# Two edits of a hand-made order on VectorE: expert picks behind the residual norm, 17 gathered rows earlier, and eight rows between digits and picks

## The chip, the core and the metric

The kernel runs on one core of one Trainium2 chip. The metric is device time in microseconds (us); lower is better. The engines are TensorE (PE in the profile; its weight loads are PEld), VectorE (DVE), ScalarE (ACT), GpSimd (POOL) and SyncE (SP), each with its own instruction stream, tied by semaphores.

## The reference

One decoder layer over 1024 tokens of width 1024. A mixer (causal pooling and a short gated convolution, one input projection and one output projection) is followed by a product-key expert retrieval:

```python
q = (xn @ w_query).reshape(T, 8, 2, 128)
s = einsum('thpc,hpkc->thpk', q, sub_keys)          # 128 keys per half
s1, i1 = top_k(s[:, :, 0], 16);  s2, i2 = top_k(s[:, :, 1], 16)
cand_s = s1[..., :, None] + s2[..., None, :]        # 256 pairs per head
top_s, pos = top_k(cand_s, 16);  idx = take_along_axis(cand_i, pos)
gates = softmax(top_s)
out[t] = sum over 8 heads x 16 picks of  gate * gelu(expert_u[idx] . x[t]) * expert_v[idx]
```

There are 16384 experts with a row of 1024 floats (4 KB) in each of expert_u and expert_v. Every token uses 128 of them.

## The kernel before

**Tokens.** Eight tiles of 128 tokens, ranked two at a time. The mixer and the queries run in four periods n = 0 to 3 of 256 tokens (two tiles each). Period n also ranks, on VectorE, the two tiles of period n - 1 (ranks 0 and 1 in period 1, 2 and 3 in period 2, 4 and 5 in period 3). Tiles 6 and 7 are ranked in the last part.

**Two ways to apply the experts.** Four tiles (ranks 0, 3, 6, 7) are gathered: for each of the 128 picks GpSimd issues one indirect DMA that fetches 128 rows of 4 KB (512 KB) into one of eight ring slots (L679), and VectorE consumes it in one unit called "row": a dot product for u rows (L1186), a multiply-add for v rows (L1197). There are 1024 rows, in the order of `ROWS`: u0, u1, v0, ... Gather r waits until row r - 8 is used. The other four tiles are dense: TensorE multiplies them with all experts (L785 scores, L831 sums, with the gate tables in between). Of these the tile of rank 1 has its gates scattered into the tables in HBM by 128 indirect DMAs of GpSimd (L650): heads 0 to 2 behind the gather `rows_by[1] + 7`, heads 3 to 7 behind the gather `rows_by[2] + 7`. `rows_by[n]` is how many rows stand in VectorE's order up to the end of period n.

**A tile's ranking on VectorE** is the list keys x4, cands, pairs x2, digits, pick, keep. "digits" (L1111 to L1130) prepares; ScalarE then makes 16 place masks (L864, `pick_places`), at a point of its own order that the planner fixes; "pick" (L1136 to L1144) waits for them (`hot_ready`); "keep" writes the expert numbers (L1170), which lets the gathers of a tile start, or the routes (L1165).

**The order on VectorE in a period.** The work of the mixer is written out, and between its steps stand places named conv0 to conv3, gate, y, y2, outp, query. `FILL[n]` gives each place an amount of us. `take(us)` fills it with the next ranking units by their `COST`, and with rows where the next unit is a pick less than 10 us (`PLACES_US`) behind its digits, or no ranking unit is left. So a period's list is fixed when the kernel is built; nothing is reordered on the chip. The steps of the mixer around it, in VectorE's order: pool_windows (L1302), conv g (L1317) with a fill ahead of each and add_x (L1335) behind the third, norm_x of the next period (L1273, L1277), conv_gate (L1343), fill gate, conv_gate, fill y, add_y (L1349, L1351), fill y2, roots_y (L1360), the residual add_half 0 and 1 (L1377), fill outp, add_half 2 and 3, norm_h x2 (L1382, L1387), fill query. TensorE's order in a period is bcv 0 to 4 (L699), the sum of squares of the next period (L710, waits for add_x), bcv 5, pa 0 and 1 of the next period (L717, waits for norm_x), pool (L728), outp 0 and 1 (L742, wait for conv_gate through ScalarE's L912), ynorm (L733, waits for add_y), outp 2 and 3, pa 2 and 3, the transposes (L748, wait for norm_h), the queries (L699), the scores (L769). It has four pairs of PSUM banks: a step also waits until the step four before it is emptied.

In the kernel before, the planner's lists are: period 1, outp: pick of tile 0; query: keep 0, keys 1 x2, cands, pairs x2, digits 1, rows 0 to 7, pick 1, keep 1, rows 8 to 10, spread (normalises the gates of the scattered tile), rows 11 to 18. Period 2, outp: pick 2; query: keep 2, keys 3 x2, cands, pairs x2, digits 3, rows 19 to 26, pick 3, keep 3, rows 27 to 39. Period 3, query: digits 4, keys 5 x4, pick 4, keep 4, cands, pairs x2, digits 5, route, rows 40 to 46, pick 5, keep 5. `rows_by` is 0, 19, 40, 47.

**Behind the periods** come 48 batches that build the gate tables, and then the dense part. There VectorE's list `order` is made of two lists: `late` (the rankings of tiles 6 and 7 with the other 977 rows between them, then weights, totals, finishes) and `items` (128 "gate" units, L1252, and 128 "sum" units, L1258, in the order in which TensorE needs them). The items are spread over `late` in proportion to its cost. `digits` is held back until the next three items are sums, or until its own pick comes.

Of the kernel before, what the change touches and what calls it, by code (L numbers as in the profile page):

```python
# [75 lines left out]


FILL = [[(f"conv{g}", 4.0) for g in range(4)] + [("gate", gate), ("y", y), ("y2", y2), ("outp", outp), ("query", query)]
        for gate, y, y2, outp, query in ((0.0, 0.0, 0.0, 0.0, 0.0), (4.0, 13.0, 6.0, 2.0, 66.0), (4.0, 13.0, 6.0, 2.0, 66.0), (0.0, 8.0, 0.0, 0.0, 66.0))]
HOT_FILL = 0.0  # L80
DENSE_SPEED = 0.99
FIRST_FILL = 42.0
# [3 lines left out]
def program(nc, hT, x_rows, w_all, sub_keys, pool_w, small, rows_g, expert_u, expert_v, uT, out):  # L86
# [57 lines left out]
    with ctx:  # L144
        def sb(name, shape, dt=FP32):
            return ctx.enter_context(nc.sbuf_tensor(name, shape, dt))
# [74 lines left out]
        gate = sb("gate", [P, HK])  # L221
# [120 lines left out]


        COST = {"keys": 6.8, "cands": 1.4, "pairs": 6.2, "digits": 3.7, "pick": 5.4, "keep": 1.2, "spread": 1.5, "route": 1.0, "row": 1.35}
        PLACES_US = 10.0

        def ranking_of(r):
            return ([("keys", r, q) for q in range(4)] + [("cands", r, 0)] + [("pairs", r, q) for q in range(2)]
# [10 lines left out]
        def take(us):  # L359
# [3 lines left out]
            while spent < us:  # L363
                row_ready = rows < 2 * HK and list(GATHERED_RANK)[rows // HK] in ranked
                if to_rank and not (to_rank[0][0] == "pick" and since_digits < PLACES_US):
                    unit = to_rank.pop(0)
# [78 lines left out]

        order, done, held = [], 0, []

        first_fill = int(np.searchsorted(np.cumsum([COST.get(u[0], 0.0) for u in late]), FIRST_FILL))
        for i, (unit, c) in enumerate(zip(late, cost)):
            if i == first_fill:  # L450
                order += items[:VJ]
                done = VJ
            if unit[0] == "pick" and held:
                order.append(held.pop())
            if unit[0] == "digits":
                held.append(unit)
            else:
                order.append(unit)
            if held and done + 2 < len(items) and all(k == "sum" for k, _, _ in items[done:done + 3]):
                order.append(held.pop())  # L460
            if i < first_fill:
                continue
            share = (c - cost[first_fill]) / (cost[-1] - cost[first_fill])
            until = min(len(items), VJ + int((len(items) - VJ) * share * DENSE_SPEED))
            order += items[done:until]
            done = until
# [1051 lines left out]
```

How the kernel before makes its waits and increments, by code:

```python
        @block.sync  # L501
# [1 line left out]
            def load_x(n):  # L503
                if n >= 2:
                    sp.wait_ge(pe_step, full(("query", n - 2, 3)))
                    if DENSE_OF[n - 2]:
                        sp.wait_ge(xfT_kept[n - 2], 16 * len(DENSE_OF[n - 2]))
                sp.dma_start(xnT[n % 2][:, :, 0:GW], hT[:, :, BASE[n] + META:BASE[n] + COLS]).then_inc(xT_loaded[n], 16)
# [3 lines left out]
            def load_w():  # L513
                k = loads[0]
                loads[0] += 1
                if k >= WSLOTS:
                    _, by, count = uses[k - WSLOTS]
                    sp.wait_ge(pe_step if by == "step" else w_freed, count)
                sp.dma_start(wslot[k % WSLOTS].rearrange("p k n -> p (k n)"), w_all[uses[k][0], :, :]).then_inc(w_loaded[k % WSLOTS], 16)
# [7 lines left out]
            sp.dma_start(poolw.rearrange("p g n -> p (g n)"), pool_w).then_inc(const_in, 16)  # L527
            sp.dma_start(skT, sub_keys).then_inc(const_in, 16)
            sp.dma_start(g_ffn, rows_g[:, 0:D]).then_inc(const_in, 16)
            for n in range(GRPS):
                for i in range(20 if n + 1 < GRPS else 18):
                    load_w()
                    if i == 0 and 2 <= n + 1 < GRPS:
                        load_x(n + 1)
            sp.wait_ge(pe_step, LAST_STEP)
            for n in range(GRPS):
                if DENSE_OF[n]:
                    sp.wait_ge(xfT_kept[n], 16 * len(DENSE_OF[n]))
# [144 lines left out]
        @block.tensor  # L685
        def _(pe):
            pe.wait_ge(const_dve, 2)
            pe.wait_ge(const_pool, 2)
```

## Time and profile before

| | |
|---|---|
| median of 3 timed runs | 2552.13 us (2550.41 to 2559.08) |
| the profiled execution | 2544.61 us, span 2542.9 us |
| TensorE busy | 2468.2 us (97%) |
| VectorE busy | 1975.3 us (78%) |
| GpSimd busy | 1438.6 us (57%) |
| ScalarE busy | 424.2 us (17%) |
| moved by DMA | 857.68 MB, 337 GB/s over the span |

A busy share is a mean over parts with different limits. The periods run from 0 to about 636 us, the table batches to about 792 us, and the dense part from 833.65 us to the end. The time between the profiled execution and its span is 1.7 us.

### The profile page before, as it was taken

The page shows a single profiled execution, that of the slowest core. Times are in us where ns is not written, and L with a number is a line of the kernel's source. Part 1 is how long each engine was busy: PE and PEld are TensorE (multiplying, and loading weights), DVE is VectorE, ACT ScalarE, POOL GpSimd, SP SyncE. Part 2 cuts the span into 40 slices and gives each one's busy share as a digit, 9 for nine tenths or more (in the row PEclk, how much of TensorE's full clock was granted, in tenths as well). Part 3 has the DMA queues.
Part 4 walks back from the last instruction along what each step waited for, and adds up shares of the span by engine and source line. Part 5 has one row for each costly group of instructions (what it writes and reads, how often), then busy time and mean ns, then how long its engine had stood idle before and what let it go on. Part 6 is the DMA issues. An engine that isn't in the chain of part 4 may idle for free.

```text
span 2542.9 us, 24120 instructions
## 1 busy us (share of the span) xinstructions
PE 2468.2 (97%) x7561; PEld 1356.1 (53%) x7561; DVE 1975.3 (78%) x4252; ACT 424.2 (17%) x782; POOL 1438.6 (57%) x1169
## 2 busy tenths in 40 slices
PE   8999999999889999999999999999999999999998
PEld 7687886868665344444444444444444444444443
DVE  4308799768888878778798877879888787888886
ACT  0213313224984000200010000000000000000001
POOL 0000276687401467577576766767676776767673
PEclk9999999999999999999999999999999999999999
DMA  8544776864868799999999999999999999999995
GB/s 333 217 158 165 307 247 191 325 164 86 264 181 277 282 379 389 386 353 406 397 372 420 420 393 399 381 411 419 420 420 402 402 402 413 417 418 419 419 420 219
DMA packets 288079, 857.68 MB, mean 337 GB/s; under 512 B 42064, under 2 KB 99408, under 8 KB 273360
## 3 DMA queue, kind: packets, MB, share of 16 engines
q0 software_dynamic: 167184, 541.73, 55.5%
q1 hardware_dynamic: 108416, 289.25, 30.1%
q10 hardware_dynamic: 12352, 25.17, 2.6%
q8 instruction: 60, 0.98, 0.1%
q14 instruction: 67, 0.55, 0.1%
HBM read 807.75 MB, written 48.30 MB: 337 GB/s over the span
## 4 chain that ended last, share of the span: by engine, by line
PE 61%; DMA 15%; POOL 13%; issue 6%; ACT 3%; DVE 1%; SPq 1%; ACTq 0%; DVEq 0%
PE pairs L831 19%; PE pairs L785 17%; PE pairs L699 15%; POOL ring L679 13%; DMA ring<-in_expert_u,idx 7%; DMA ring<-in_expert_v,idx 6%; PE pairs L742 4%; PE pairs L717 2%; ACT arena L985 2%; PE pairs L769 1%; PE pairs L798 1%; ACT arena L1009 1%; DMA arena<-gate_tables 1%; DVE arena L1197 1%; ACT arena L987 0%
## 5 line engine op out<-in xcount | busy, mean ns | idle before, releaser
L679 POOL DMA_INDIRECT ring<-in_expert_u,idx x512 | 644.7, 1259 | 626.2 <-DVE dots L1186 355.5
L831 PE MATMUL pairs<-arena 128*128 128x512 f32 x2048 | 888.7, 595 | 15.0 <-DVE arena L1252 13.2
L785 PE MATMUL pairs<-arena 128*128 128x512 f32 x2048 | 882.5, 592 | 0.0
L1186 DVE CUSTOM_DVE_ANT_0 junk<-ring,xf 128x1024 bf16<-128x1024 f32 x512 | 612.0, 1223 | 163.4 <-DMA ring<-in_expert_u,idx 159.9
L679 POOL DMA_INDIRECT ring<-in_expert_v,idx x512 | 581.2, 1135 | 265.9 <-issue 119.9
L831 PEld LDWEIGHTS pairs<-arena 128*128 128x128 f32 x2048 | 390.5, 191 | 510.8 <-issue 507.9
L785 PEld LDWEIGHTS pairs<-arena 128*128 128x128 f32 x2048 | 388.6, 190 | 486.5 <-issue 486.5
L1197 DVE SCALAR_TENSOR_TENSOR arena<-ring,arena 128x1024 f32<-128x1024 f32 x381 | 475.6, 1284 | 96.0 <-DMA ring<-in_expert_v,idx 94.8
L699 PE MATMUL pairs<-arena 128*128 128x256 f32 (+1 forms) x1792 | 393.2, 382 | 5.9 <-ACT arena L946 4.7
L699 PEld LDWEIGHTS pairs<-arena 128*128 128x128 f32 x1792 | 341.2, 191 | 55.9 <-ACT arena L946 5.4
L993 ACT ACTIVATE arena<-pairs 128x512 f32<-128x512 f32 x128 | 76.1, 597 | 1068.0 <-PE pairs L785 1042.2
L650 POOL DMA_INDIRECT gate_tables<-gate,place x128 | 206.0, 1609 | 51.9 <-issue 38.7
L1197 DVE SCALAR_TENSOR_TENSOR xf<-ring,arena,xf 128x1024 f32<-128x1024 f32 x126 | 156.6, 1283 | 24.8 <-DMA ring<-in_expert_v,idx 24.7
L1467 DVE TENSOR_SCALAR arena<-iota,arena 128x128 f32<-128x128 f32 x384 | 101.3, 344 | 25.5 <-PE pairs L798 25.5
L798 PE MATMUL pairs<-arena 128*128 128x128 f32 x768 | 91.4, 277 | 28.0 <-ACT arena L1009 25.3
L742 PE MATMUL pairs<-arena 128*128 128x512 f32 x256 | 111.2, 592 | 0.0
L798 PEld LDWEIGHTS pairs<-arena 128*128 128x128 f32 x768 | 88.2, 192 | 34.0 <-issue 30.9
L1258 DVE TENSOR_TENSOR arena<-arena,pairs 128x512 f32<-128x512 f32 x128 | 87.0, 680 | 18.1 <-PE pairs L831 17.7
L1252 DVE TENSOR_TENSOR arena<-arena 128x512 f32<-128x512 f32 x128 | 87.5, 687 | 14.7 <-DMA arena<-gate_tables 11.6
L864 ACT ACTIVATE pick_all<-digit,place 128x256 bf16<-128x256 f32 x128 | 80.4, 721 | 51.9 <-DVE digit L1130 51.9
L742 PEld LDWEIGHTS pairs<-arena 128*128 128x128 f32 x256 | 48.6, 190 | 57.8 <-issue 55.0
L1062 DVE MAX8 tops<-arena 128x8 f32<-128x128 f32 x112 | 24.5, 280 | 62.0 <-ACT arena L961 60.4
(174 smaller groups left out, 1059.2 us busy)
## 6 DMA issues: line engine op xcount, KB each, us to landing
arena<-in_w_all SPq DMA_DIRECT2D x80, 1024.0 KB, 6.6
arena<-in_uT SPq DMA_DIRECT2D x128, 512.0 KB, 6.7
arena<-in_expert_v SPq DMA_DIRECT2D x128, 512.0 KB, 9.0
arena<-gate_tables SPq DMA_DIRECT2D x32, 1024.0 KB, 10.0
gate_tables<-arena SPq DMA_DIRECT2D x11, 2048.0 KB, 9.1
gate_tables<-junk ACTq DMA_DIRECT2D x4, 2048.0 KB, 13.8
ring<-in_expert_u,idx POOLq DMA_INDIRECT x512, 9.0
ring<-in_expert_v,idx POOLq DMA_INDIRECT x512, 9.6
```

What stands on the lines that cost most here:

```text
L650: nc.gpsimd.indirect_dma_start(out=g_flat, out_offset=bass.IndirectOffsetOnAxis(ap=place[:, k:k + 1], axis=0), in_=gate[:, k:k + 1], in_of ...
L679: nc.gpsimd.indirect_dma_start(out=ring[:, r % RING, :], out_offset=None, in_=expert_u if table == "u" else expert_v, in_offset=bass.Indir ...
L699: last = nc.tensor.matmul(out_, w[:, k, c * P:(c + 1) * P], xn[:, k, :], start=(k == 0), stop=(k == KD - 1))
L742: last = nc.tensor.matmul(pair[:, q * 512:(q + 1) * 512], yT[:, NG * (1 - half) + k, t * P:(t + 1) * P], w_out[q].rearrange("p k n -> p (k ...
L785: last = nc.tensor.matmul(score_bank[x], uslot[:, x % USLOTS, k * P:(k + 1) * P], xfT[:, k, :], start=(k == 0), stop=(k == KD - 1))
L798: last = nc.tensor.matmul(g_bank[(2 * b + m) % 4][:, q * KEYS:(q + 1) * KEYS], hots[:, c, 0, 4 * m + q, :], hots[:, c, 1, 4 * m + q, :], s ...
L831: last = nc.tensor.matmul(o_bank[n % 4], gated[:, x % GSLOTS, t * P:(t + 1) * P], vrows[:, j, half * 512:(half + 1) * 512], start=(j == 0) ...
L1186: nc.vector.tensor_tensor_reduce(out=junk[:, r % 2, :], in0=row, in1=xf[:, t % 2, :], scale=1.0, scalar=0.0, op0=ALU.mult, op1=ALU.add, ac ...
L1197: nc.vector.scalar_tensor_tensor(out=to[:, k % 2, :], in0=row, scalar=weight[:, k:k + 1], in1=h2 if k == 0 else to[:, k % 2, :], op0=ALU.m ...
L1252: nc.vector.tensor_tensor(s, s, gtab[a // GJ % 2][:, :, a % GJ, :], ALU.mult).then_inc(w_ready, 1)
L1258: nc.vector.tensor_tensor(piece, piece, o_bank[b % 4], ALU.add).then_inc(o_added, 1)
L1467: last = nc.vector.tensor_scalar(hots[:, c, 1, t, :], iota[:], routeT[:, 1, k:k + 1], routeT[:, 2, k:k + 1], ALU.is_equal, ALU.mult)
```

## The change

Two numbers of `FILL` change in periods 1 and 2 (outp 2.0 to 0.0; query 66.0 to 82.0 and 84.0), and the loop that makes `order` holds a pick back until eight rows stand behind its digits, with its keep behind it.

```diff
 FILL = [...
-        for gate, y, y2, outp, query in ((0.0, 0.0, 0.0, 0.0, 0.0), (4.0, 13.0, 6.0, 2.0, 66.0), (4.0, 13.0, 6.0, 2.0, 66.0), (0.0, 8.0, 0.0, 0.0, 66.0))]
+        for gate, y, y2, outp, query in ((0.0, 0.0, 0.0, 0.0, 0.0), (4.0, 13.0, 6.0, 0.0, 82.0), (4.0, 13.0, 6.0, 0.0, 84.0), (0.0, 8.0, 0.0, 0.0, 66.0))]
...
-        PLACES_US = 10.0
+        PLACES_US, PLACES_ROWS = 10.0, 8
...
+        pick_late, rows_since = [], 0
...
             if unit[0] == "pick" and held:
                 order.append(held.pop())
+                rows_since = 0
+            rows_since += unit[0] == "row"
             if unit[0] == "digits":
                 held.append(unit)
+            elif unit[0] == "pick" and rows_since < PLACES_ROWS or unit[0] == "keep" and pick_late:
+                pick_late.append(unit)
             else:
                 order.append(unit)
+            if rows_since >= PLACES_ROWS:
+                order += pick_late
+                pick_late = []
             if held and done + 2 < len(items) and all(k == "sum" for k, _, _ in items[done:done + 3]):
                 order.append(held.pop())
+                rows_since = 0
```

## Rows read from the trace of the kernel before

**Rows 1.** The page: the span, and the busy time of each engine.
```profile
span 2542.9 us, 24120 instructions
PE 2468.2 (97%) x7561; PEld 1356.1 (53%) x7561; DVE 1975.3 (78%) x4252; ACT 424.2 (17%) x782; POOL 1438.6 (57%) x1169
```

**Rows 2.** Busy by window (us, PE, PEld, DVE, ACT, POOL, clock, DMA, GB/s).
```profile
834.00:2161.00 1327.00, 1324.42 (x3078) 585.20 (x3077) 1079.29 (x1714) 89.65 (x145) 903.21 (x753) 1.00 0.99 393
```

**Rows 3.** Waits of PE from 834 us: us in total, times, longest.
```profile
PE pairs L831 <- DVE arena L1252: 13.2, 6, 6.2
PE pairs L831 <- DVE arena L1258: 1.1, 1, 1.1
```

**Rows 4.** Timeline of PE, two stretches of 114 sums (start, us, idle before).
```profile
1718.75 49.16 PE L831 MATMUL pairs<-arena 128*128 128x512 f32 x114 [0.54 <-DVE arena L1252]
...
2482.85 51.70 PE L831 MATMUL pairs<-arena 128*128 128x512 f32 x114 [4.31 <-DVE arena L1252]
```

**Rows 5.** Busy by window, gathers of line 679 on POOL alone.
```profile
833.60:2482.80 1649.20, 1127.46 (x944) 1.00 1.00 398
```

**Rows 6.** Timeline of DVE, period 1: picks, residual, digits, last row.
```profile
255.33 2.28 DVE L1136 TENSOR_TENSOR pick_all<-topf,pick_all 128x4096 bf16<-128x4096 bf16 x1
...
260.99 1.28 DVE L1377 SCALAR_TENSOR_TENSOR arena<-pairs,ycol,arena 128x1024 f32<-128x1024 f32 x1
262.50 1.28 DVE L1377 SCALAR_TENSOR_TENSOR arena<-pairs,ycol,arena 128x1024 f32<-128x1024 f32 x1 [0.22 <-PE pairs L742]
...
290.91 0.29 DVE L1130 TENSOR_TENSOR digit<-pos,pick_all 128x128 f32<-128x128 uint32 x1
...
311.26 2.29 DVE L1136 TENSOR_TENSOR pick_all<-topf,pick_all 128x4096 bf16<-128x4096 bf16 x1 [10.58 <-ACT pick_all L864]
...
330.85 1.22 DVE L1186 CUSTOM_DVE_ANT_0 junk<-ring,xf 128x1024 bf16<-128x1024 f32 x1
```

**Rows 7.** Timeline of ACT: the place masks of tile 1.
```profile
301.25 9.98 ACT L864 ACTIVATE pick_all<-digit,place 128x256 bf16<-128x256 f32 x16
```

**Rows 8.** Ring, POOL, 325 to 338.6 us: ns, starts; landing.
```profile
L679 POOL DMA_INDIRECT ring<-in_expert_u,idx x8: 946/1140/1988, 325.2 to 337.4; - x8
...
DMA to landing us min/median/max: 6.2/14.7/17.3
```

**Rows 9.** Timeline of DVE, period 2: norm_x, add_y.
```profile
373.49 1.75 DVE L1273 RECIPROCAL arena<-arena 128x256 f32<-128x256 f32 x1 [1.67 <-ACT arena L927]
...
399.37 0.69 DVE L1351 TENSOR_TENSOR arena<-arena 128x512 f32<-128x512 f32 x1
```

**Rows 10.** Timeline of PE, period 2: sum of squares, ynorm.
```profile
370.88 1.03 PE L710 MATMUL pairs<-arena,ones 128*128 128x256 f32 x4
...
401.01 1.03 PE L733 MATMUL pairs<-arena,ones 128*128 128x256 f32 x4
```

**Rows 11.** Timeline of DVE: pick 3, last row, conv_gate of period 3.
```profile
465.06 2.29 DVE L1136 TENSOR_TENSOR pick_all<-topf,pick_all 128x4096 bf16<-128x4096 bf16 x1 [10.56 <-ACT pick_all L864]
...
489.45 1.23 DVE L1186 CUSTOM_DVE_ANT_0 junk<-ring,xf 128x1024 bf16<-128x1024 f32 x1 [4.01 <-DMA ring<-in_expert_u,idx]
...
532.42 0.76 DVE L1343 TENSOR_TENSOR arena<-arena 128x256 f32<-128x256 f32 x2 [3.73 <-ACT arena L935]
```

**Rows 12.** Ring, POOL, 482.8 to 493 us.
```profile
L679 POOL DMA_INDIRECT ring<-in_expert_u,idx x8: 934/938/1097, 482.9 to 491.8; - x8
...
DMA to landing us min/median/max: 7.5/7.6/7.7
```

**Rows 13.** Timeline of PE: the queries of periods 2 and 3.
```profile
426.23 55.49 PE L699 MATMUL pairs<-arena 128*128 128x256 f32 x256 [1.80 <-ACT arena L946]
...
566.45 1.94 PE L748 MATMUL pairs<-ident,arena 128*128 128x128 f32 x8 [3.76 <-DVE arena L1387]
569.55 57.24 PE L699 MATMUL pairs<-arena 128*128 128x256 f32 x256 [1.16 <-issue]
```

**Rows 14.** Timeline of DVE, dense part: pick 6.
```profile
1074.63 2.29 DVE L1136 TENSOR_TENSOR pick_all<-topf,pick_all 128x4096 bf16<-128x4096 bf16 x1 [5.72 <-ACT pick_all L864]
```

## Prediction, made before the changed kernel was run

> **What bounds the kernel now.** The page first: TensorE is busy for 97% of the span, VectorE for 78% [rows 1]. That is a mean over parts, so I split it. By windows, TensorE is busy for 1324.42 of 1327 us of the dense part from 834 to 2161 us [rows 2], and its waits from 834 us on name only VectorE's gate and sum units: 13.2 + 1.1 us, of which 6.2 us are the start of the part, where the first gates load [rows 3]. So 8.1 us are all that VectorE and the gathered rows cost TensorE in the dense part. The timeline adds one price: the longest of these waits, 4.31 us, ends at 2482.85 us, and the 114 matmuls behind it take 51.70 us where the same 114 take 49.16 us behind a wait of 0.54 us [rows 4], 2.5 us more. The dense part can give back 8.1 + 2.5 = 10.6 us, whatever happens to the rows. The rows themselves are close behind: 944 gathers in 1649.2 us, 1.75 us each [rows 5], about as long as TensorE's own list. The two lines are in step, and the rows' line has no large reserve on TensorE's.
>
> In the periods ahead of it (0 to 636 us) TensorE waits just as little, but here VectorE is the engine that is level with it. I read that from VectorE's timeline in period 2, from the end of period 1's list on. The last row of period 1 starts at 330.85 us and lasts 1.22 us, and the mixer's work of period 2 follows it at 332.0 [rows 6]. From there to add_y I find one wait, 1.67 us ahead of norm_x; add_y ends at 399.37 + 0.69 = 400.06 us [rows 9], and TensorE takes up ynorm, which needs it, at 401.01 [rows 10], 0.95 us later. (The sum of squares, at 370.88, and pa lie between and move with it.) VectorE's reserve in period 2 is 1.67 + 0.95 = 2.6 us. Any more lateness passes to TensorE, and TensorE has no idle time later in which to win it back. In period 3 the one wait is 3.73 us ahead of the conv_gate that outp needs [rows 11].
>
> **The change, part by part.**
>
> *Which units move.* I work the planner's list out by hand. With outp at 0.0 the pick of tile 0 (2) and its keep go to the head of the query list. Period 1, amount 82: 5.4 + 1.2 + 13.6 + 1.4 + 12.4 + 3.7 = 37.7 to the end of digits, 8 rows of 1.35 = 48.5, pick and keep 55.1, 3 rows and spread 60.65, then 16 rows to 82.25. That is 27 rows for 19. Period 2, amount 84: 37.7, 8 rows, pick, keep = 55.1, then 22 rows: 30 for 21. `rows_by` becomes 0, 27, 57, 64. The extra rows, 8 and 9, all stand behind the second pick of their period. None stands between a digits and its pick, where there are eight as before, because `PLACES_US` is as it was.
>
> *The pick behind the residual.* Pick 0 takes from 255.33 to 260.99 us, 5.7 us. Behind it add_half 3 still waits 0.22 us for TensorE, at 262.50 [rows 6]. So the pick fills a wait for TensorE now. Taken away, that wait grows by 5.7 us, norm_h ends where it did, and the transposes start no earlier. The 5.7 us then stand ahead of digits 1, which end at 290.91 + 0.29 + 5.7 = 296.9 us. ScalarE starts its masks at 301.25 and is done at 311.2 [rows 7], at a place of its own order that does not move. So pick 1 starts at 311.26 as before, and its wait of 10.58 us shrinks to about 4.9. The same in period 2, where pick 3 waits 10.56 us [rows 11]. This edit is worth 0. If the cover were gone it would cost 5.7 us; a gain is excluded because TensorE's outp 3 sets add_half 3.
>
> *Eight more rows in period 1.* They are rows 19 to 26, at 1.22 us each on VectorE [rows 6]: 9.8 us at the least. But their data must be there, and for this the trace of before has the exact price, since it issues the same eight gathers at the same time, for the next period: starts from 325.2 to 337.4 us, landing 6.2 us behind the issue for the quickest and 17.3 for the slowest [rows 8]. They grow with time, so the last lands at 337.4 + 17.3 = 354.7, is used by 355.9, and VectorE reaches period 2's mixer at 355.9 for 332.0: 23.9 us late. Ends: 9.8 and 23.9; I take 23.9, since these are the same transfers. The mixer's loads in front of them are not moved. Less the reserve of 2.6 us this costs TensorE 21.3 us.
>
> The Trainium skill, "DMA: Bandwidth & Descriptors" (section "Queues, rings and completion order"), says that each DMA engine takes turns, packet by packet, between the queues that have work. By it, eight gathers behind the weight loads would share evenly with them and not be served last, and a slow landing is the two loads' bytes together. It leaves the term between its ends; the 17.3 us [rows 8] beside 7.7 us in the quieter stretch [rows 12] agree with it.
>
> *Nine more rows in period 2.* Pick 3 is tied to ScalarE's masks and so to TensorE, and moves with it. The list ends at 489.45 + 1.23 = 490.7 us [rows 11]. The next eight gathers start between 482.9 and 491.8 and land in 7.5 to 7.7 us [rows 12]: the last at about 499.4. The ninth can be issued once the first is used, at about 493, and lands at 500.9; used by 502.1. That is 11.4 us late (at the least 9 x 1.22 = 11.0; at the most, with landings as slow as in period 1, 9 x 23.9 / 8 = 26.9). Less the wait of 3.73 us in period 3 [rows 11]: 7.7 us for TensorE.
>
> *The clock.* The new stalls come where TensorE was continuous. Behind the wait of 3.76 us at 566.45 the 256 query matmuls take 57.24 us, against 55.49 in period 2 [rows 13]: 1.75 us. In period 2 such a loss is covered, as VectorE is later still; in period 3 it is not. I add 1.75 once (ends 0 and 3.5).
>
> *The scatter and the queues.* No DMA is added. GpSimd's 128 scatters start behind gathers 34 and 64 instead of 26 and 47, so some 20 to 30 us later, and still end ahead of the table batches' last store. 0 (if not covered, up to the 24 us by which period 1 is late). SP's and ScalarE's orders are as before.
>
> *17 rows fewer in the dense part.* 17 x 1.75 = 29.8 us off the rows' line [rows 5]. TensorE can take only its 10.6 us of that, and I give it all (ends 0 and 10.6).
>
> *Eight rows between digits and pick.* Pick 6 waits 5.72 us for the masks [rows 14], with three rows behind its digits; five more rows fill that. By the proportions pick 7 has over eight rows anyway. In that stretch TensorE never waits, so it is 5.7 us more room for the rows' line and 0 in the sum. Ends 0 and 5.7, and inside the 10.6.
>
> **The sum.** 21.3 + 7.7 + 1.75 = 30.7 us lost in the periods, 10.6 regained: +20.1 us. On the profiled execution's own 2544.6 us: 2564.7. The timed runs' median lies 7.5 us above that execution. If the excess is spread over everything, the new median is 2552.1 + 20.1 = 2572.2; if it is the rows' line, slower than in the profile, the new 35 us of room removes it: 2564.7. I can't tell from one trace, and take the middle: **2568 us**.
>
> **Rivals.**
> - *Rows at VectorE's pace.* If the gathers land soon enough, period 1 is late by 9.8 us only: TensorE loses 7.2 there and 11.0 - 3.7 = 7.3 in period 3, 14.5; less 10.6 is +3.9, or 2549 to 2556 us. For it: the rows of period 2 land in 7.7 us [rows 12]. Against: the landings of period 1's own gathers [rows 8].
> - *Faster: the rows fit.* The picks of periods 1 and 2 wait 10.58 and 10.56 us [rows 6, 11], which is room for 17 rows, and the dense part is worth more than the profile shows (10.6 + 7.5). If VectorE's lateness stopped short of TensorE at add_y [rows 9, 10], the time would be 2552.1 - 18.1 = 2534 us. It decides from a loss in the periods below about 10 us. Against it: the extra rows stand behind the picks in a fixed order, so they can't use the waits, and 17 x 1.22 = 20.7 us of VectorE's work meet 2.6 + 3.7 us of reserve.
> - *Worse: period 2's rows land like period 1's.* 26.9 - 3.7 = 23.2 for 7.7: +35.6, 2580 to 2588 us. For it: the load queue is filled a weight piece at a time in every period.
> - *It doesn't do what it says.* The waits that the rows should fill are ahead of the picks. This I hold true already and have in the sum.
>
> The Trainium skill, "SBUF — State Buffer" (section "Who interferes with whom"), says that a VectorE instruction with two SBUF inputs blocks a GpSimd instruction that reads SBUF. Here gathers last 1988 ns at most and 946 at least in one stretch [rows 8]. If this were the limit and not the landing, eight rows at 1.99 + 0.30 us would make 18.3 us, and the loss 5.6 us less; that lies between my case and the first rival.
>
> **How the numbers follow.** My case (+10 to +28): 0.64. Rows at VectorE's pace: 0.17. Worse: 0.11. Faster: 0.08. The measurement can tell 0.3% from no change, 7.7 us here: 2544.5 to 2559.8. The faster case lies below it for the most part, 0.07. The first rival lies within it, with a little of my own case: 0.16. Slower: 0.77. Range: from the middle of the first rival, 2553, to the start of the worse case, 2582; about 2 in 10 lie outside.
>
> **What would show it.** Right: in period 1 the rows behind pick 1 wait for their gathers, and the mixer of period 2 starts near 356 us; TensorE stands idle at the sum of squares, pa and ynorm of period 2, 21 us in all, and 8 us at outp of period 3; the dense part starts about 30 us later, near 864, and then TensorE hardly waits. Wrong: if pool_windows of period 2 starts before 345 us, if TensorE's waits between 333 and 560 us stay under 10 us, or if the dense part is shorter by over 11 us.

## The result

The changed kernel takes 2571.75 us (median of 5 runs, 2568.78 to 2575.23) against 2550.79 us for the kernel before (5 runs, 2546.96 to 2559.08). The ratio is 1.0074, 95% interval 1.0056 to 1.0091: slower by 19 us (14 to 23 us) by the ratio, by 21 us by the medians. The forecast was 2568 us, with a range of 2553 to 2582. The profiled execution took 2568.78 us (before: 2544.61). For the kernel before that is below all its five timed runs, for the changed one it is the lowest of the five. What compares two timelines below compares one execution with one.

The page of the changed kernel, span and engines, stands beside [rows 1]:

```profile
span 2567.1 us, 24121 instructions
PE 2468.2 (96%) x7561; PEld 1356.9 (53%) x7561; DVE 1972.5 (77%) x4252; ACT 426.2 (17%) x783; POOL 1436.6 (56%) x1169
```

The matmuls are the same, and TensorE's busy time is the same to a tenth of a us. The span grew by 24.2 us, so by the page all of it is waiting. (That the busy times agree so closely is chance: a slower clock lengthens the matmuls behind the new waits, and in the dense part the same 3928 matmuls take 1688.5 us where they took 1692.8.) The waits of PE in the changed kernel (us in total, times, longest), first in the periods, 183 to 660 us, and below the dots from 860 us on [rows 3]:

```profile
PE pairs L720 <- DVE arena L1347: 17.9, 1, 17.9
PE pairs L752 <- ACT arena L922: 11.4, 1, 11.4
PE pairs L709 <- ACT arena L956: 4.1, 2, 2.3
PE pairs L758 <- DVE arena L1397: 3.8, 1, 3.8
PE pairs L779 <- ACT arena L960: 2.4, 2, 1.2
PE pairs L743 <- DVE arena L1361: 1.6, 1, 1.6
...
PE pairs L841 <- DVE arena L1262: 6.5, 1, 6.5
PE pairs L841 <- ACT arena L1003: 0.7, 1, 0.7
```

(Lines from 445 on have moved by 10: L720 is the sum of squares, L752 outp, L743 ynorm, L841 the sums.) Two long waits are new, and one group is gone. The 6.5 us are the first gates of the dense part, and the 0.7 us stand ahead of them, ending at 860.05 us. Behind the first gates TensorE waits for nothing, where it waited for 8.1 us [rows 3].

VectorE's timeline of the changed kernel in period 1 and at the start of period 2 (start, us, [idle before]); it answers to [rows 6]:

```profile
262.13 1.28 DVE L1387 SCALAR_TENSOR_TENSOR arena<-pairs,ycol,arena 128x1024 f32<-128x1024 f32 x1 [5.51 <-PE pairs L752]
...
266.86 2.29 DVE L1146 TENSOR_TENSOR pick_all<-topf,pick_all 128x4096 bf16<-128x4096 bf16 x1
...
311.55 2.29 DVE L1146 TENSOR_TENSOR pick_all<-topf,pick_all 128x4096 bf16<-128x4096 bf16 x1 [5.28 <-ACT pick_all L874]
...
332.29 1.22 DVE L1196 CUSTOM_DVE_ANT_0 junk<-ring,xf 128x1024 bf16<-128x1024 f32 x1
337.97 1.22 DVE L1196 CUSTOM_DVE_ANT_0 junk<-ring,xf 128x1024 bf16<-128x1024 f32 x1 [4.46 <-DMA ring<-in_expert_u,idx]
341.70 1.23 DVE L1196 CUSTOM_DVE_ANT_0 junk<-ring,xf 128x1024 bf16<-128x1024 f32 x1 [2.49 <-DMA ring<-in_expert_u,idx]
345.10 1.23 DVE L1196 CUSTOM_DVE_ANT_0 junk<-ring,xf 128x1024 bf16<-128x1024 f32 x1 [2.17 <-DMA ring<-in_expert_u,idx]
...
355.69 1.23 DVE L1196 CUSTOM_DVE_ANT_0 junk<-ring,xf 128x1024 bf16<-128x1024 f32 x1 [1.09 <-DMA ring<-in_expert_u,idx]
```

The pick has left the residual, and add_half 3 now waits 5.51 us for TensorE where it waited 0.22. Pick 1 starts at 311.55 for 311.26. From 332.29 to 356.9 us VectorE works on the last eight rows, and seven of them wait for their gathers. VectorE's waits for gathers from 332 us to 426 us in one line:

```profile
DVE junk L1196 <- DMA ring<-in_expert_u,idx: 14.8, 7, 4.5
```

TensorE's timeline of the changed kernel, for [rows 10] and [rows 13]:

```profile
389.12 2.04 PE L720 MATMUL pairs<-arena,ones 128*128 128x256 f32 x4 [17.92 <-DVE arena L1347]
390.96 8.59 PE L709 MATMUL pairs<-arena 128*128 128x256 f32 x32
...
423.52 1.10 PE L743 MATMUL pairs<-arena,ones 128*128 128x256 f32 x4 [1.61 <-DVE arena L1361]
...
449.73 55.49 PE L709 MATMUL pairs<-arena 128*128 128x256 f32 x256 [2.27 <-ACT arena L956]
...
568.40 15.52 PE L752 MATMUL pairs<-arena 128*128 128x512 f32 x32 [11.42 <-ACT arena L922]
...
606.25 56.88 PE L709 MATMUL pairs<-arena 128*128 128x256 f32 x256 [1.16 <-issue]
...
870.19 54.27 PE L841 MATMUL pairs<-arena 128*128 128x512 f32 x120 [6.47 <-DVE arena L1262]
```

Step by step against the kernel before: ynorm of period 2 is late by 423.52 - 401.01 = 22.5 us, the queries of period 2 by 23.5, those of period 3 by 36.7, the dense part by 870.19 - 833.65 = 36.5 us. From there to the end it is 1696.9 us for 1709.3: 12.3 us regained. 36.5 - 12.3 = 24.2 us is the difference of the spans.

The split into 36.5 and 12.3 is less sure than its sum. The kernel with the gap alone (below) has the periods' list of the kernel before, and in its profile the dense part starts at 842.96 us, 9.3 us later than 833.65, and lasts 1720.3 us, 11.1 us longer.

### The profile page after: what moved, and what is told of

The parts are those of the page before. It is cut to its first block, busy times and chain, and to the rows that moved or that the text cites. A ratio compares the mean times of both kernels' runs of the same rounds, so it can differ in the third digit from the quotient of the medians.

```text
span 2567.1 us, 24121 instructions
## 1 busy us (share of the span) xinstructions
PE 2468.2 (96%) x7561; PEld 1356.9 (53%) x7561; DVE 1972.5 (77%) x4252; ACT 426.2 (17%) x783; POOL 1436.6 (56%) x1169
## 4 chain that ended last, share of the span: by engine, by line
PE 85%; DVE 5%; ACT 4%; DMA 2%; issue 1%; POOL 1%; SPq 1%; ACTq 0%; DVEq 0%
PE pairs L841 34%; PE pairs L795 33%; PE pairs L709 10%; PE pairs L752 4%; PE pairs L727 2%; ACT arena L995 2%; POOL ring L689 1%; DMA ring<-in_expert_u,idx 1%; PE pairs L808 1%; ACT arena L1019 1%; DMA arena<-gate_tables 1%; ACT pick_all L874 1%; PE pairs L779 1%; DVE topi L1083 0%; DVE topi L1075 0%
## 5 line engine op out<-in xcount | busy, mean ns | idle before, releaser
L841 PE MATMUL pairs<-arena 128*128 128x512 f32 x2048 | 884.4, 593 | 7.2 <-DVE arena L1262 6.5
L689 POOL DMA_INDIRECT ring<-in_expert_v,idx x512 | 574.5, 1122 | 287.7 <-DVE arena L1207 140.8
L841 PEld LDWEIGHTS pairs<-arena 128*128 128x128 f32 x2048 | 389.9, 190 | 499.2 <-issue 497.8
L752 PE MATMUL pairs<-arena 128*128 128x512 f32 x256 | 113.1, 599 | 11.6 <-ACT arena L922 11.4
L1262 DVE TENSOR_TENSOR arena<-arena 128x512 f32<-128x512 f32 x128 | 87.5, 687 | 30.4 <-ACT arena L1003 17.9
L752 PEld LDWEIGHTS pairs<-arena 128*128 128x128 f32 x256 | 49.1, 193 | 71.0 <-issue 67.1
```

The source lines that it names most:

```text
L689: nc.gpsimd.indirect_dma_start(out=ring[:, r % RING, :], out_offset=None, in_=expert_u if table == "u" else expert_v, in_offset=bass.Indir ...
L752: last = nc.tensor.matmul(pair[:, q * 512:(q + 1) * 512], yT[:, NG * (1 - half) + k, t * P:(t + 1) * P], w_out[q].rearrange("p k n -> p (k ...
L841: last = nc.tensor.matmul(o_bank[n % 4], gated[:, x % GSLOTS, t * P:(t + 1) * P], vrows[:, j, half * 512:(half + 1) * 512], start=(j == 0) ...
L1262: nc.vector.tensor_tensor(s, s, gtab[a // GJ % 2][:, :, a % GJ, :], ALU.mult).then_inc(w_ready, 1)
```

## The experiments

The theory: the extra rows stand behind the second pick, where the gathers are slow and VectorE is level with TensorE; the moved pick and the gap are worth nothing. All ratios are to the kernel before, timed on the same chip, with the 95% interval; 0.001 is 2.6 us.

**Pick moved, rows as before** (e1_pick_only).

```diff
-(4.0, 13.0, 6.0, 2.0, 66.0), (4.0, 13.0, 6.0, 2.0, 66.0)
+(4.0, 13.0, 6.0, 0.0, 71.4), (4.0, 13.0, 6.0, 0.0, 71.4)
```

> Only the first picks of periods 1 and 2 move behind the residual; rows_by stays 0, 19, 40, 47. Late-rows theory: the pick used a wait for TensorE, so it is worth nothing: TensorE's waits in the periods stay at about 11 us, the wait of pick 1 shrinks from 10.6 to about 5, and the time is that of before within 3 us. Rival, the moved pick is what costs: its 5.7 us in each of two periods reach TensorE, +6 to +11 us. Rival, it brings something (residual earlier): -2 to -5 us.

Measured 1.0017 (1.0001 to 1.0033). In its trace no wait of TensorE for VectorE is new in the periods, and pick 1 waits for 5.34 us at 312.25:

```profile
312.25 2.29 DVE L1136 TENSOR_TENSOR pick_all<-topf,pick_all 128x4096 bf16<-128x4096 bf16 x1 [5.34 <-ACT pick_all L864]
```

The trace shows no cost; the timing leaves between 0 and 8 us. So the moved pick brings nothing. The rival's cost of 6 to 11 us has no wait in the trace to stand on, but the interval excludes only its upper half.

**Rows only** (e2_rows_only): the query amounts 76.6 and 78.6 with outp left at 2.0, the old loop in the dense part.

```diff
-(4.0, 13.0, 6.0, 2.0, 66.0), (4.0, 13.0, 6.0, 2.0, 66.0)
+(4.0, 13.0, 6.0, 2.0, 76.6), (4.0, 13.0, 6.0, 2.0, 78.6)
```

> Only the 8 and 9 extra rows; the picks stay between the residual halves and the dense part has the old loop. Late-rows theory: the whole loss is here, TensorE late by about 36 us at the table batches, dense part 10 to 12 us shorter: +19 to +24 us. Rival, the moved pick costs: only +10 to +15 us here. Rival, the gap of eight rows in the dense part is what gives the regained 12 us: then this one is +30 to +36 us.

Measured 1.0081 (1.0058 to 1.0104): the whole loss. Its waits of PE in the periods and, below the dots, from 840 us on:

```profile
PE pairs L710 <- DVE arena L1337: 17.0, 1, 17.0
PE pairs L742 <- ACT arena L912: 9.3, 1, 9.3
...
PE pairs L831 <- DVE arena L1252: 6.6, 1, 6.6
PE pairs L831 <- issue: 0.7, 1, 0.7
```

The same two waits, and the same calm dense part without the gap of eight rows. The rows are both the loss and the gain.

**Gap only** (e3_gap_only): the new loop of `order`, `FILL` as before.

```diff
-        PLACES_US = 10.0
+        PLACES_US, PLACES_ROWS = 10.0, 8
...
```

> Only the gap of eight rows between digits and pick in the dense part. Late-rows theory: the wait of 5.7 us at pick 6 goes, no TensorE time in that stretch depends on it; but the rows' line gets 5.7 us of room, and where it is what TensorE waits for later, part of 8.1 us goes: 0 to -6 us. Rival, the gap brings nothing because the gathers set the rows' pace: 0 within 1 us. Rival, the gap is part of the loss: +2 or more.

Measured 0.9995 (0.9978 to 1.0013), -6 to +3 us: no difference, the rival's 0 as well as the theory's 0 to -6. In its trace pick 6 has no wait any more. From 840 us on TensorE still waits for VectorE, more than in the trace of before [rows 3]:

```profile
PE pairs L841 <- DVE arena L1262: 19.6, 6, 6.5
PE pairs L841 <- DVE arena L1268: 4.4, 3, 1.9
```

**VectorE's time without the gathers** (e4_no_gather): eight dot products of the same length behind period 1's list, on data in SBUF, their results dropped.

```diff
             def fill(n, where):
...
+                if (n, where) == (1, "query"):
+                    dve.drain()
+                    for k in range(8):
+                        nc.vector.tensor_tensor_reduce(out=junk[:, k % 2, :], in0=xf[:, 0, :], in1=xf[:, 0, :], scale=1.0, scalar=0.0,
+                                                       op0=ALU.mult, op1=ALU.add, accum_out=ycol[:, 2, 0:1])
+                        dve.drain()
```

> The kernel before with eight extra dot products of row length at the end of period 1's list, on data that is there already (their results are dropped). It separates VectorE's time from the gathers' landing. Late-rows theory: about 8 x 1.2 = 9.8 us (a little more with a drain each) less a reserve of 2.6: TensorE late by 7 to 8 us at the queries of period 2, and the time +5 to +9 us, against 23.5 us late in the changed kernel. Rival, the landing plays no part and it is VectorE's or the port's time: as late as with the real rows, over 20 us.

Measured 1.0031 (1.0015 to 1.0046), +4 to +12 us. VectorE and then TensorE in its trace:

```profile
341.84 1.23 DVE L1272 CUSTOM_DVE_ANT_0 junk<-xf 128x1024 bf16<-128x1024 f32 x1
343.15 0.44 DVE L1308 TENSOR_TENSOR arena<-arena 128x271 f32<-128x271 f32 x1
```

```profile
345.54 27.86 PE L699 MATMUL pairs<-arena 128*128 128x256 f32 x128 [1.92 <-DMA arena<-in_w_all]
...
435.97 55.49 PE L699 MATMUL pairs<-arena 128*128 128x256 f32 x256 [1.79 <-ACT arena L946]
```

The mixer's work starts 11.1 us late, not 24.9, and the queries 435.97 - 426.23 = 9.7 us late, not 23.5. The expectation was 7 to 8. The wait of 1.92 us for a weight load adds nothing to it, since TensorE waits for VectorE behind it, at the sum of squares and at ynorm:

```profile
PE pairs L710 <- DVE arena L1343: 2.2, 1, 2.2
PE pairs L733 <- DVE arena L1357: 2.0, 1, 2.0
```

ynorm starts at 410.23 us, 9.2 us late for 11.1 us of VectorE. So of the 23.5 us of the real rows about two fifths is VectorE's time and three fifths the landing. The 14.8 us that VectorE waits for gathers in the changed kernel say the same: 24.9 - 14.8 = 10.1 us are work. The rival, over 20 us without any gather, is out.

**One period at a time** (e5_period1: query 76.6 and 66.0; e6_period2: 66.0 and 78.6).

```diff
-(4.0, 13.0, 6.0, 2.0, 66.0), (4.0, 13.0, 6.0, 2.0, 66.0)
+(4.0, 13.0, 6.0, 2.0, 76.6), (4.0, 13.0, 6.0, 2.0, 66.0)      e5
+(4.0, 13.0, 6.0, 2.0, 66.0), (4.0, 13.0, 6.0, 2.0, 78.6)      e6
```

> Only period 1's eight extra rows (27 there, 21 in period 2 as before). Late-rows theory: TensorE late by about 23 us at the queries of period 2 and by no more after that; eight rows fewer in the dense part regain 8 to 11 us; +12 to +15 us. Rival, one period's lateness is absorbed by the reserve of the next: under +5 us.

> Only period 2's nine extra rows. Late-rows theory: TensorE late by 8 to 13 us at outp of period 3 (7.7 was predicted, 11.4 plus 1.6 of clock measured in the changed kernel, where period 1 had moved as well); dense regains 8 to 11 us; 0 to +4 us. If the lateness is 7.7 here and 11 there, the larger one comes from what period 1 shifts, otherwise from the supply of gathers itself.

Measured 1.0051 (1.0033 to 1.0068) for period 1's eight, 1.0011 (0.9996 to 1.0026) for period 2's nine. In us that is +13 (8 to 17) and +3 (-1 to +7), both as the theory had them. In the trace with period 1's rows the queries of period 2 start at 449.64 us, 23.4 late. For period 2's rows, outp of period 3 in TensorE's timeline, and the nine gathers of rows 40 to 48:

```profile
545.35 16.13 PE L742 MATMUL pairs<-arena 128*128 128x512 f32 x32 [10.18 <-ACT arena L912]
```

```profile
L679 POOL DMA_INDIRECT ring<-in_expert_u,idx x9: 933/940/1721, 484.7 to 496.3; - x9
...
DMA to landing us min/median/max: 7.6/8.6/9.8
```

The wait is 10.2 us and the clock behind it costs 16.13 - 13.90 = 2.2 us (granted clock 0.86 in outp, 1.00 in the kernel before). Period 1's list is as before here, so the 7.7 us that I predicted were too few by the supply of gathers itself. The last of the nine starts at 496.3 us and lands 9.8 us later. I had it start at 493 and land at 500.9, from eight gathers that had taken 7.5 to 7.7 us [rows 12].

**Rows into the waits** (e7_wait12 and its repeat e11_wait12_again: 12 rows between digits and pick in periods 1 and 2; e8_wait16: 16; e9_wait12_16: 12 in period 1 and 16 in period 2; e10_wait_gap: that with the change's gap in the dense part). `take` gets the time to keep between digits and pick as an argument:

```diff
-        def take(us):
+        def take(us, gap):
...
-                if to_rank and not (to_rank[0][0] == "pick" and since_digits < PLACES_US):
+                if to_rank and not (to_rank[0][0] == "pick" and since_digits < gap):
...
-                plan[n, where] = take(us)
+                plan[n, where] = take(us, {1: 16.0, 2: 16.0}.get(n, PLACES_US))      e7; {1: 16.0, 2: 21.5} e9, e10; 21.5 twice e8
...
-                        exp_after = step_at(n, where, spent)
+                        exp_after = ("query", 1, 2)      e8 alone
...
-(4.0, 13.0, 6.0, 2.0, 66.0), (4.0, 13.0, 6.0, 2.0, 66.0)
+(4.0, 13.0, 6.0, 2.0, 71.4), (4.0, 13.0, 6.0, 2.0, 71.4)      e7; 71.4 and 76.8 e9, e10; 76.8 twice e8
```

> Four more rows in each of periods 1 and 2, placed between digits and pick (12 for 8), so inside the wait of 10.6 us; the picks as before. Late-rows theory: they cost nothing in the periods (TensorE waits as in the kernel before), since the wait covers 4 x 1.2 us and the gathers go out before the next load burst; eight rows fewer in the dense part: -5 to -9 us. Rival, every extra row ahead of the dense part costs: 0 to +8 us.

> Eight more rows in each of periods 1 and 2, all between digits and pick (16 for 8), ScalarE's exponential held at its old place; nearly as many rows moved as by the change (16 against 17). Late-rows theory: the last gathers of the sixteen land near 313 to 316 us, so pick 1 is 2 to 5 us late, about as much as the reserve of 2.6 and 3.7 us: TensorE loses 0 to 3 us, dense regains 10 to 12: -7 to -11 us. Rival, every extra row costs as in the change: +15 to +24 us.

> 12 rows between digits and pick in period 1, 16 in period 2 (8 in the kernel before), picks in their old place, old dense loop: 12 rows moved ahead, none behind a second pick. With 16 in both periods TensorE lost some 9 us in period 2 (sum of squares, ynorm and the clock behind them) and nothing in period 3. Late-rows theory: the loss of period 2 is gone with 12 there, and the reserve of period 3 takes the 16: periods as before, dense part with 12 rows fewer, -13 to -17 us, a little better than 12 and 12. Rival, what counts is only how many rows leave the dense part and 8 are enough: the same as 12 and 12, -12 us. Rival, the longer waits for gathers in period 2 reach TensorE after all: -5 us.

> The one with 12 and 16 rows between digits and pick, and the change's gap of eight rows in the dense part. Alone, the gap made no difference. Late-rows theory: the same as without the gap within 2 us, since the rows' line already has room of 12 x 1.75 us. Rival, once the periods cost nothing the gap's 5.7 us count: 3 to 6 us below it.

> The one with 12 and 12 rows once more, beside the two others on the same chip: -11 to -14 us against the kernel before, if the first measurement holds.

| rows between digits and pick | rows moved | ratio (95%) |
|---|---|---|
| 12, 12 | 8 | 0.9949 (0.9931 to 0.9967) |
| 12, 12, repeat | 8 | 0.9963 (0.9947 to 0.9980) |
| 16, 16 | 16 | 0.9961 (0.9947 to 0.9975) |
| 12, 16 | 12 | 0.9949 (0.9930 to 0.9968) |
| 12, 16, and the gap | 12 | 0.9958 (0.9940 to 0.9976) |

All five beat both kernels and lie 9 to 13 us below the kernel before. The 12 and 12 brought 13 us at first (8 to 18) where 5 to 9 were expected, and 9 in the repeat. 16 and 16 brought 10, as expected, and 12 and 16 brought 13, at the lower end of what was expected; its rival, no better than 12 and 12, is not excluded. The gap again adds nothing that the intervals can show. VectorE in the one with 12 and 12, from its last row ahead of pick 1 to period 2:

```profile
310.74 1.23 DVE L1186 CUSTOM_DVE_ANT_0 junk<-ring,xf 128x1024 bf16<-128x1024 f32 x1 [4.96 <-DMA ring<-in_expert_u,idx]
312.57 2.29 DVE L1136 TENSOR_TENSOR pick_all<-topf,pick_all 128x4096 bf16<-128x4096 bf16 x1 [0.60 <-ACT pick_all L864]
...
332.17 1.22 DVE L1186 CUSTOM_DVE_ANT_0 junk<-ring,xf 128x1024 bf16<-128x1024 f32 x1
333.32 0.43 DVE L1302 TENSOR_TENSOR arena<-arena 128x271 f32<-128x271 f32 x1
```

The wait of 10.58 us has gone into four rows, 4 x 1.15 = 4.6 us, and their waits for gathers, the longest 4.96 us. Pick 1 waits 0.60 us, and period 2 starts at 333.3, 1.3 us late. With 16 in both periods it is too much for period 1: pick 1 starts at 317.50 us, 6.2 us late, where 2 to 5 had been expected. TensorE is 9.6 us late at the queries of period 2, with these waits:

```profile
PE pairs L710 <- DVE arena L1337: 3.5, 1, 3.5
...
PE pairs L733 <- DVE arena L1351: 2.0, 1, 2.0
```

With 12 and 16 these two are gone and one of 1.0 us at outp of period 3 has come. The four versions can't be told apart by their times; 12 and 16 had the lowest median of its batch, 2538.37 us against 2550.31. Nearly the same number of rows costs 21 us when 17 stand behind the picks and brings 10 us when 16 stand ahead of them.

## Why the prediction was right, step by step

- *Reserve of VectorE in period 2 (2.6 us).* Right. Its lateness of 24.9 us (356.9 for 332.0) came out as 22.5 us at ynorm, 24.9 - 2.4. The eight dot products without gathers come near it: 11.1 us in, 9.2 out at ynorm, 1.9 less.
- *The moved pick (0).* Right in the trace (5.51 us of wait where the pick was, pick 1 within 0.3 us). The time of the kernel with this edit alone allows 0 to 8 us.
- *Period 1's rows (23.9 us late on VectorE, 21.3 on TensorE).* Right: 24.9 and 22.5, 23.5 at the queries. The landings of the next period's gathers in the trace of before were those of the moved rows: these start from 325.5 to 338.4 us, and the last lands 17.3 us after its start. The last start is 1.0 us later than I had it, and that is the 1.0 us by which 23.9 was short. GpSimd's issuing beside VectorE's rows, my 18.3 us, is not the limit: the last of the eight is issued 17.3 us before its row is used. The first rival, rows at VectorE's pace, is the no-gather kernel: 9.2 us at ynorm, not 22.5.
- *Period 2's rows (7.7 us).* The term of the sum that was mis-sized: "the last at about 499.4. The ninth can be issued once the first is used, at about 493". Measured 568.40 - 533.32 - 23.5 = 11.6 us in the changed kernel, and a wait of 10.2 with this part alone. There the last of the nine gathers started at 496.3 us, 3.3 later than I had it (1.7 of them because the period itself ran later), and landed in 9.8 us; in the changed kernel the last landed in 10.5. I had read the landings, 7.5 to 7.7 us, where no gathers followed. That it is the following gathers and weight loads that slow them was not tried by itself.
- *Clock (1.75 us).* Right. 15.52 - 13.90 = 1.6 us at outp of period 3: behind the wait the granted clock was 0.50 for the first 2.6 us, that is 1.2 GHz of 2.4, and 0.90 over the 32 matmuls. In period 2 the 36 matmuls behind the wait of 17.92 us took 2.5 us more, and ynorm waited 1.61 us for VectorE behind that: covered, as said.
- *Dense part (10.6 us).* 12.3 us, over the 11 us that I had named as a sign of being wrong, which was drawn too tight. TensorE's waits behind the first gates went from 8.1 us to none, and the other 4.3 us are matmuls that ran shorter, 1688.5 us for 1692.8. I had priced that at 2.5, from the longest wait alone. In the profiles of the other kernels with all 977 rows this part lasts 5 to 11 us longer than in the one that I read, so the 12.3 us are rather too few than too many.
- *The gap (0 in the sum).* Not contradicted: 0.9995, -6 to +3 us.
- *The sum.* +20.1 us was forecast for the profile and 24.2 measured there: 36.5 for 30.7 lost, 12.3 for 10.6 regained. Both terms were too small, and as their signs are opposite the errors cancel in part. Of the 5.8 us that the loss was short, 3.9 are period 2's rows, and 2.2 had arisen by the queries of period 2.
- *The signs.* The mixer of period 2 started at 356.8 us (near 356 forecast), TensorE's waits there were 17.9 + 1.6 us (21), at outp of period 3 11.4 (8), and the dense part started at 870 (near 864).
- *The timed runs.* I left open whether the 7.5 us by which the median stood above the profiled execution were the rows' line. Profiles of other kernels that have all 977 rows there point to it: TensorE's waits behind the first gates are 17.5 us with the gap alone, 15.3 with the pick alone and 11.8 with the dot products, against 8.1 in the profile of before and none with 17 rows fewer. That fits a timed difference (+21.0) below that of the profiles (+24.2). That a typical run of the kernel before waits 12 to 18 us is inferred from three profiles, not shown for the timed runs.
- *The number.* 2568 for 2571.75 us is in part luck. It was the middle between 2564.7 and 2572.2 us. If the excess is the rows' line, as it seems, my own sum said 2564.7 and was 7 us short.
- *The faster rival, "the rows fit".* It named what really is to be had: with the rows ahead of the pick they do fit, and the kernel gains 9 to 13 us. In the change they stood behind it.

## What to carry to other kernels

A wait on an in-order engine is filled only by what stands in front of the waiting instruction. Units added behind it are paid in full, and from the point where that engine's reserve against the bounding engine ends, one for one. The price of a prefetched unit placed earlier is the landing of its data at that place, and the trace of before may have it, as here, in the transfer that already stands at that place; where the change makes such transfers follow each other more closely, take the slow end of their landings. A stage that bounds only now and then (8 to 18 us of 1700 here) gives back little more than those waits and the slower matmuls behind them, however much work is taken out of it.

## What the runs showed that I had not expected

- Eight rows (4 MB) fewer in the dense part give most of what there is: 8, 12 and 16 moved rows measure alike. With 8 moved, TensorE's waits there are 4.0 + 1.2 us behind the first gates, with 12 moved 2.0. The profiles do show each step, one execution each, as the time from the first 120 sums to the end: 1709.3 to 1720.3 us with all rows, 1703.5 to 1705.3 with 8 or 9 fewer, 1698.7 to 1700.8 with 12 or 16 fewer, 1696.9 and 1697.0 with 17 fewer.
- In nine of the eleven experiments TensorE waits 1.1 to 4.5 us for a weight load at about 345 us, which the profile of before does not show:

```profile
348.94 30.76 PE L709 MATMUL pairs<-arena 128*128 128x256 f32 x128 [4.52 <-DMA arena<-in_w_all]
```

This is the kernel with the gap alone, whose list is that of before at this place, so the change to the kernel does not make the wait. The 128 matmuls behind it take 30.76 us, where they take 27.86 behind the wait of 1.92 us in the no-gather kernel. At that place gathers take up to 17.3 us to land [rows 8], and which of the loads and gathers is late differs from profile to profile; what decides it was not tried. Such a wait, 3.9 us in the kernel with 12 and 12 rows, is one reason why the gain of 9 to 13 us shows in the timed runs and not in the profiled spans (2544.8 us there, 2542.9 before).
